# The end of the recurrence turn in another order: mean sums behind the chain, the eight-row state turned in the third tile, the fourth gate by halves

## The chip, the cores and the metric

The kernel runs on one core of a Trainium2 chip. The metric is the device time of one execution in microseconds (us), fp32 data in and out. The times given are medians of a few executions.

## The reference, cut to what matters

The program is one inference step of a hybrid recurrent decoder layer with width 2048. It serves 16 meta tokens with a prompt of 512 tokens, and 8 sample sequences of 4 tokens each: 560 token columns in all. The work that the change touches is the RWKV-7 branch and the gated merge after it:

```python
z = rms_norm(x) @ w_in              # r, k, v, gate za, merge gates ga, gb are column blocks of z
xs = zf + (prev - zf) * mu          # token shift
# per head of 64 channels, per token:
sa = S @ a_t
S = S * w_t + sa * b_t + v_t * k_t  # matrix state
y = S @ r_t
...
mean = mean(y); var = mean((y - mean)**2)          # per head
y = (y - mean) * rsqrt(var + LNX_EPS) * lnx_w + lnx_b
y = (y + bonus) * silu(za)
m = sigmoid(ga) * y + sigmoid(gb) * ob             # ob comes from the GLA branch
x = x + rms_norm(m @ w_out)
```

The final states of the prompt (one) and of the samples (eight) are outputs too.

## The kernel before

All 2048 channels are cut into 16 pairs of heads, 128 channels each. The recurrence stage makes one turn for each pair: `turn_of` is written once for every engine, 15 turns run in a hardware loop (`Fori`) and the last one (`last=True`) stands alone. Every engine works through its own instruction list in order; semaphores (`wait_ge`, `then_inc`) tie the lists together. There is no planner. The order is written by hand.

**The projections are the filling.** Each turn needs six columns tiles of `z`: t = 0 is the key, 1 the receptance r, 2 the value, 3 the gate za, 4 the merge gate ga, 5 the merge gate gb. Tiles 6, 7 and 8 are the key, r and value of the next turn. A tile is a product of 128 weight columns with 560 tokens over 2048 rows, in two token halves of 280. A half has 16 **steps**, and a step (`Projection.steps`, lines 353 to 371) is three matmuls (lines 363, 364, 365), because every fp32 product is split in high and low parts. The parts of the weights are made tile by tile: SyncE loads 1 MB into `raw` in two halves, ScalarE rounds it (`split_hi`, line 341), VectorE subtracts (`split_lo`, line 349). There are two sets of `w_hi` and `w_lo`, used in turn, and one `raw`. Half 0 of a tile always goes to PSUM bank 0 and half 1 to bank 1. Before step 0 of a half, TensorE waits until the half before it in that bank has been read out (`evacuated`), and for the first half also until `split_lo` of the tile is done:

```python
if k == 0:
    pe.wait_ge(self.lo.sem, self.lo.at(i, 2 * t + 2))
    pe.wait_ge(self.evacuated.sem, self.evacuated.at(i, 2 * t - 1 + half))
```

Tiles 0 to 2 and 6 to 8 are read out by ScalarE copies into a shift buffer (`evacuate`, that is `to_shift_buffer`, lines 381, 384, 386); tiles 3 to 5 by ScalarE tanh (`tanh_gate_of`, line 1571) with a VectorE product behind it (lines 1732, 1773, 1810).

**The recurrence stands between the steps.** `run(n)` issues n steps of the filling; between two of them TensorE does a piece of the recurrence whose input the other engines made meanwhile. From the start of tile 4 a turn has 128 steps of filling (tiles 4 to 7); the last turn has 64 (tiles 4 and 5). The order is: the eight sample states (the "eight-row" state) are transposed (line 1903) and copied to `s8` by ScalarE (line 1576); Gram matrices (1923); v transposed (1929); products; a matrix inverse by squarings (1937) with ScalarE copies (1602) and VectorE sums (1766, 1768, 1779, 1782, 1784); the maps (2030, 2040, 2047); the chain over the nine chunks (2071); and the outputs y (2077, 2082).

**The end of the turn**, after y: ScalarE copies y to SBUF (1623, 1625). TensorE forms `s8`'s increment (2089), the sums of y over each head (`head_sums`, 1881, `mean_done`), and the sums of squares (1881 again, `var_done`); VectorE subtracts the mean (1834), ScalarE squares (1631) and takes the root (1646), VectorE divides and merges (1840 to 1850) and GpSimd stores the result. The nine final states are transposed on TensorE (2103), copied by ScalarE (`states_out`, 1639) and stored by GpSimd (1497, 1499). The copies of tiles 6 and 7, the splits of tiles 7 and 8 and the token shift of the next key (`shift_key`, 392 to 400) stand between these.

## Time and profile before

| | before |
|---|---|
| median of 3 runs | 3549.05 us (3548.31 to 3569.71) |
| profiled execution, its own time | 3559.79 us |
| its span, first to last instruction | 3558.3 us |
| TensorE matmul busy | 3279.7 us, 92% |
| VectorE busy | 1721.4 us, 48% |
| ScalarE busy | 1054.2 us, 30% |
| GpSimd busy | 395.8 us, 11% |

A row of the view in order of time gives start, length, engine, line, operation and, in square brackets, how long the engine had been idle and who released it. A row can merge several instructions of one line (x8). The matmul records overlap: one projection matmul is recorded as 0.29 us long and the next starts 0.13 us after it, so that a recorded idle time is shorter than the time lost. Lines that end a wait are those of the instruction that released it. The recurrence stage lies between about 1160 and 3280 us of the span.

### The profile page before, as it was taken

To read this page: it belongs to the slowest core of one execution; us is meant where nothing else is said; L and a number is where in the kernel's file an instruction comes from. 1 tells how busy PE (TensorE), PEld (TensorE's weight loads), DVE (VectorE), ACT (ScalarE), POOL (GpSimd) and SP (SyncE) were. 2 spreads that over 40 slices of the span, in tenths; PEclk is the share of its full clock that TensorE was granted. 3 is DMA by queue.
4 is the path that set the end of the run, shared out by engine and by line. 5 is a ranking of instruction groups with operands and counts; after the bars stand their busy time and mean duration, and the time that the engine had idled before them with its cause. 6 is when DMAs were issued, how large, how long until landed. Compare 5 with 4: busy or idle time off the path is not lost. (4 is left out here: it accounts for less than half of the span.)

```text
span 3558.3 us, 82556 instructions
## 1 busy us (share of the span) xinstructions
PE 3279.7 (92%) x33471; PEld 3028.9 (85%) x33471; DVE 1721.4 (48%) x2447; ACT 1054.2 (30%) x1680; POOL 395.8 (11%) x795
## 2 busy tenths in 40 slices
PE   3899999999997899999999999999999999996796
PEld 3798898898994889988988998998989998895796
DVE  3254454354443445655654654654654654563324
ACT  3232232332320322332332332432332332331222
POOL 2100100100001201110110110110110110111000
PEclk6899898998995999999999999999999999998898
DMA  2222323323313212221221221311221221221422
GB/s 86 71 79 72 125 73 91 119 60 103 106 36 108 71 53 56 74 55 45 75 62 38 74 63 43 80 51 49 75 62 49 64 62 50 61 61 42 150 75 97
DMA packets 368508, 255.10 MB, mean 72 GB/s; under 512 B 19412, under 2 KB 347600, under 8 KB 366288
## 3 DMA queue, kind: packets, MB, share of 16 engines
q1 hardware_dynamic: 342592, 184.18, 18.9%
q0 software_dynamic: 25600, 66.02, 5.8%
q8 instruction: 282, 4.62, 0.5%
q14 instruction: 34, 0.28, 0.0%
HBM read 212.69 MB, written 37.45 MB: 70 GB/s over the span
## 5 line engine op out<-in xcount | busy, mean ns | idle before, releaser
L363 PE MATMUL psum<-act_hi,w_hi 128*128 128x280 f32 (+3 forms) x5216 | 1613.2, 309 | 89.8 <-DVE w_lo L349 38.7
L365 PE MATMUL psum<-act_hi,w_lo 128*128 128x280 f32 (+3 forms) x5216 | 1539.9, 295 | 0.0
L364 PE MATMUL psum<-act_lo,w_hi 128*128 128x280 f32 (+3 forms) x5216 | 1539.1, 295 | 0.0
L363 PEld LDWEIGHTS psum<-act_hi,w_hi 128*128 128x128 f32 (+2 forms) x5216 | 999.6, 192 | 162.7 <-issue 107.0
L364 PEld LDWEIGHTS psum<-act_lo,w_hi 128*128 128x128 f32 (+2 forms) x5216 | 999.0, 192 | 6.0 <-issue 1.0
L365 PEld LDWEIGHTS psum<-act_hi,w_lo 128*128 128x128 f32 (+2 forms) x5216 | 998.3, 191 | 1.1
L349 DVE TENSOR_TENSOR w_lo<-raw,w_hi 128x1024 fp32r<-128x1024 f32 (+1 forms) x326 | 396.6, 1217 | 320.9 <-ACT w_hi L341 306.4
L341 ACT CAST w_hi<-raw 128x1024 fp32r<-128x1024 f32 (+1 forms) x326 | 340.1, 1043 | 87.4 <-DMA raw<-in_w_in_dram 36.5
L1937 PE MATMUL psum<-arena 64*64 64x64 f32 x9216 | 309.4, 219 | 6.6 <-DVE arena L1782 6.5
L1937 PEld LDWEIGHTS psum<-arena 64*64 64x64 f32 x9216 | 286.1, 134 | 32.9 <-issue 32.9
L1497 POOL DMA_DIRECT2D out_s_rwkv_dram<-arena x128 | 78.9, 624 | 1558.5 <-ACT arena L1639 1558.4
L1602 ACT COPY arena<-psum 128x576 f32<-128x576 f32 x80 | 51.4, 643 | 280.6 <-PE psum L1937 280.6
L1571 ACT ACTIVATE arena<-psum 128x280 f32<-128x280 f32 x96 | 39.0, 406 | 307.6 <-PE psum L365 306.6
L677 ACT COPY arena<-psum 128x280 f32<-128x280 f32 x48 | 18.9, 394 | 315.0 <-PE psum L365 314.9
L946 DVE SCALAR_TENSOR_TENSOR arena<-arena,psum 128x512 f32<-128x512 f32 x64 | 47.9, 748 | 101.6 <-PE psum L1214 100.4
L384 ACT COPY arena<-psum 128x248 f32<-128x248 f32 (+1 forms) x50 | 18.4, 367 | 264.7 <-PE psum L365 264.7
L1214 PE MATMUL psum<-arena 48*128 48x512 f32 x128 | 85.2, 798 | 6.5 <-DVE arena L939 6.5
L1815 DVE SCALAR_TENSOR_TENSOR arena<-psum,arena 128x64 f32<-128x64 f32 x128 | 36.3, 284 | 111.2 <-PE psum L2071 111.1
L2254 DVE COPY arena<-psum 128x256 f32 (+1 forms) x32 | 13.6, 425 | 145.7 <-PE psum L2300 145.7
L1203 PEld LDWEIGHTS psum<-arena 128*128 128x128 f32 x512 | 73.5, 227 | 11.8 <-issue 11.8
L635 POOL DMA_DIRECT2D out_s_gla_dram<-arena x32 | 23.0, 718 | 529.8 <-DVE arena L946 529.8
L1463 POOL DMA_DIRECT2D arena<-in_state_rwkv_dram x128 | 75.6, 599 | 47.6 <-issue 43.8
(312 smaller groups left out, 3513.8 us busy)
## 6 DMA issues: line engine op xcount, KB each, us to landing
raw<-in_w_in_dram SPq DMA_DIRECT2D x288, 512.0 KB, 4.6
arena<-in_state_gla_dram POOLq DMA_DIRECT2D x32, 512.0 KB, 5.3
out_s_gla_dram<-arena POOLq DMA_DIRECT2D x32, 512.0 KB, 3.3
raw<-in_w_out_dram SPq DMA_DIRECT2D x32, 512.0 KB, 4.5
ob_dram<-arena POOLq DMA_DIRECT2D x16, 280.0 KB, 3.1
arena<-ob_dram POOLq DMA_DIRECT2D x16, 280.0 KB, 5.8
m_dram<-arena POOLq DMA_DIRECT2D x16, 280.0 KB, 2.4
arena<-m_dram SPq DMA_DIRECT2D x4, 1120.0 KB, 12.2
```

The lines of the kernel that those rows point to most:

```text
L341: nc.scalar.copy(w_hi[t % 2][:, ks, 0:width], raw[half][:, :, 0:width]).then_inc(self.hi.sem, 1)
L349: eng.tensor_tensor(w_lo[t % 2][:, ks, 0:width], raw[half][:, :, 0:width], w_hi[t % 2][:, ks, 0:width].bitcast(F32), SUB).then_inc(self.lo ...
L363: pe.matmul(out, hi, act_hi[:, k, cols], start=(k == 0), stop=False)
L364: pe.matmul(out, hi, act_lo[:, k, cols], start=False, stop=False)
L365: mm = pe.matmul(out, lo, act_hi[:, k, cols], start=False, stop=(k == KT - 1))
L946: stt(out=sstate[s % 3][:, n, :], in0=sstate[s % 3][:, n, :], scalar=ends[:, n, GN + s:GN + s + 1], in1=bank[4 + n], op0=MUL, op1=ADD).the ...
L1203: m = mm(o8[n][:, TAIL + s * TS:TAIL + (s + 1) * TS], sstate[s % 3][:, k, kv(n)], q_8[k][:, s * TS:(s + 1) * TS], start=False, stop=False, ...
L1214: m = mm(bank[4 + n], kd_seq[0:LAST, kv(n)], v_rows[0:LAST, GF, :], start=True, stop=True)
L1463: pool.dma_start(state8_in[0:C, s, :].rearrange("v (h k) -> v h k", h=2), state_rwkv[0, s, ds(2 * i, 2)].rearrange("h v k -> v h k")).then ...
L1497: pool.dma_start(s_rwkv[0, s, ds(2 * i, 2)].rearrange("h v k -> v h k"), state_out[0:C, s, :].rearrange("v (h k) -> v h k", h=2)).then_inc ...
L1602: nc.scalar.copy(out, psum[:, b:b + 2, :].rearrange("p b x -> p (b x)")[:, 0:NC * C].rearrange("p (c t) -> p c t", c=NC)).then_inc(signal. ...
L1937: m = mm(out, left(c)[head[h]], right(c)[head[h]], start=True, stop=True)
```

## The change

It reorders; it adds and removes no arithmetic.

- **Third tile.** On TensorE the eight state transposes move from behind all 32 steps of tile 3 to behind its step 16, that is between its two halves. ScalarE copies them to `s8` between the two tanh of that tile.
- **Fourth gate by halves.** ScalarE takes the tanh of tile 4's half 0 earlier, behind the second of three copies of the inverse, and half 1 at the old place. VectorE does the product of half 0 behind the third sum of the inverse (`gate_second(0)`), and half 1 behind the fourth.
- **End of the turn, TensorE.** Before: 4 steps, s8 product, 10 steps, mean sums, 20 steps, 8 of 9 state transposes, square sums, 6 steps, the last transpose, the other 13 steps. After: 6 steps, mean sums, s8 product, 8 steps, square sums, 14 steps, 8 transposes, 6 steps, the last one, the other 19 steps.
- **End of the turn, ScalarE.** Before: y copies, split 7, read-out of tile 6, square, split 8, states 0 and 1, root, state 2, read-out of tile 7. After: split 7, y copies, square, root, read-out of tile 6, split 8, states 0, 1, 2, read-out of tile 7.
- **End of the turn, VectorE.** Before: s8 sum and scaling, split 7, centring, split 8, key shift, division and merge. After: centring, split 7, s8, division and merge, split 8, key shift.

```diff
--- before.py
+++ after.py
@@ -1565,16 +1565,17 @@
                     act.wait_ge(exps.sem, exps.next(i))
                     pd.split_hi(act, i, mine, 4)
 
-                    def tanh_gate_of(t, out):
-                        for half in range(2):
+                    def tanh_gate_of(t, out, halves=(0, 1)):
+                        for half in halves:
                             act.wait_ge(pd.half.sem, pd.half.at(i, 2 * t + half + 1))
                             nc.scalar.activation(out[:, half * HALF:(half + 1) * HALF], bank[half][:, 0:HALF], ACT.Tanh, scale=0.5).then_inc(tanh_gate.sem, 1)
                             act.wait_ge(tanh_gate.sem, tanh_gate.next(i))
-                    tanh_gate_of(3, tg)
-
+                    tanh_gate_of(3, tg, (0,))
                     act.wait_ge(s8_turned.sem, s8_turned.at(i, 1))
                     nc.scalar.copy(s8, bank[6].rearrange("p (s v) -> p s v", s=NSEQ)).then_inc(s8_ready.sem, 1)
                     act.wait_ge(s8_ready.sem, s8_ready.next(i))
+                    tanh_gate_of(3, tg, (1,))
+
                     for g in range(3):
                         act.wait_ge(v_turned.sem, v_turned.at(i, g + 1))
                         cs, src = (slice(4 * g, 4 * g + 4), bank[4 + g]) if g < 2 else (slice(NF, NC), bank[4][:, 0:P])
@@ -1605,7 +1606,9 @@
                     for n, out in enumerate((x2, n_d, x2)):
                         act.wait_ge(inv_mm.sem, inv_mm.at(i, n + 1))
                         to_sbuf(out, 6, inv_a)
-                    tanh_gate_of(4, tg)
+                        if n == 1:
+                            tanh_gate_of(4, tg, (0,))
+                    tanh_gate_of(4, tg, (1,))
                     if not last:
                         pd.split_hi(act, i, mine, 6)
                     for n in range(2):
@@ -1618,34 +1621,34 @@
                     nc.scalar.copy(uv[0:C, :, 0:C], pq[:, :, C:P]).then_inc(p_ready.sem, 1)
                     act.wait_ge(p_ready.sem, p_ready.next(i))
                     tanh_gate_of(5, tg)
+                    if not last:
+                        pd.split_hi(act, i, mine, 7)
                     act.wait_ge(y_state.sem, y_state.at(i, 1))
                     act.wait_ge(stored.sem, stored.at(i, 0))
                     nc.scalar.copy(y_t[:, 0:NF * C], bank[7]).then_inc(mine.sem, 1)
                     act.wait_ge(mine.sem, mine.next(i))
                     nc.scalar.copy(y_t[:, NF * C:T], bank[6][:, C:C + LAST]).then_inc(y_ready.sem, 1)
                     act.wait_ge(y_ready.sem, y_ready.next(i))
-                    if not last:
-                        pd.split_hi(act, i, mine, 7)
-                        evacuate(act, i, mine, 6)
                     act.wait_ge(centred.sem, centred.at(i, 1))
                     nc.scalar.activation(e_t, y_t, ACT.Square).then_inc(squared.sem, 1)
                     act.wait_ge(squared.sem, squared.next(i))
-                    if not last:
-                        pd.split_hi(act, i, mine, 8)
-
-                    def states_out(n):
-                        act.wait_ge(out_turned.sem, out_turned.at(i, n + 1))
-                        w = 4 if n < 2 else 1
-                        nc.scalar.copy(state_out[0:C, 4 * n:4 * n + w, :], bank[2 + n % 2][0:C, 0:w * P].rearrange("p (s k) -> p s k", s=w)).then_inc(out_read.sem, 1)
-                        act.wait_ge(out_read.sem, out_read.next(i))
-                    states_out(0)
-                    states_out(1)
                     act.wait_ge(var_done.sem, var_done.at(i, 1))
                     for half in range(2):
                         signal = root if half else mine
                         nc.scalar.activation(e_t[:, half * HALF:(half + 1) * HALF], bank[6 + half][:, 0:HALF], ACT.Sqrt,
                                              scale=1.0 / HEAD, bias=tiny[:, 1:2]).then_inc(signal.sem, 1)
                         act.wait_ge(signal.sem, signal.next(i))
+
+                    def states_out(n):
+                        act.wait_ge(out_turned.sem, out_turned.at(i, n + 1))
+                        w = 4 if n < 2 else 1
+                        nc.scalar.copy(state_out[0:C, 4 * n:4 * n + w, :], bank[2 + n % 2][0:C, 0:w * P].rearrange("p (s k) -> p s k", s=w)).then_inc(out_read.sem, 1)
+                        act.wait_ge(out_read.sem, out_read.next(i))
+                    if not last:
+                        evacuate(act, i, mine, 6)
+                        pd.split_hi(act, i, mine, 8)
+                    states_out(0)
+                    states_out(1)
                     states_out(2)
                     if not last:
                         evacuate(act, i, mine, 7)
@@ -1760,18 +1763,21 @@
 
                         op(slice(0, NC), lambda b: psum[:, b:b + 2, :].rearrange("p b x -> p (b x)")[:, 0:NC * C].rearrange("p (c t) -> p c t", c=NC)).then_inc(signal.sem, 1)
                         dve.wait_ge(signal.sem, signal.next(i))
+                    def gate_second(half):
+                        dve.wait_ge(tanh_gate.sem, tanh_gate.at(i, half + 3))
+                        pd.evacuated.count = 8 + half
+                        cols = slice(half * HALF, (half + 1) * HALF)
+                        stt(out=gate[:, cols], in0=tg[:, cols], scalar=1.0, in1=gate[:, cols], op0=ADD, op1=MUL).then_inc(pd.evacuated.sem, 1)
+                        dve.wait_ge(pd.evacuated.sem, pd.evacuated.next(i))
                     for n in range(4):
                         dve.wait_ge(inv_mm.sem, inv_mm.at(i, n + 1))
                         if n < 2:
                             both(lambda c, b: dve.tensor_copy((t2, t_d)[n][:, c, :], b(4)), inv_b)
                         if n > 0:
                             both(lambda c, b: tt(inv[:, c, :], inv[:, c, :], b(2), ADD), inv_b)
-                    for half in range(2):
-                        dve.wait_ge(tanh_gate.sem, tanh_gate.at(i, half + 3))
-                        pd.evacuated.count = 8 + half
-                        cols = slice(half * HALF, (half + 1) * HALF)
-                        stt(out=gate[:, cols], in0=tg[:, cols], scalar=1.0, in1=gate[:, cols], op0=ADD, op1=MUL).then_inc(pd.evacuated.sem, 1)
-                        dve.wait_ge(pd.evacuated.sem, pd.evacuated.next(i))
+                        if n == 2:
+                            gate_second(0)
+                    gate_second(1)
                     if not last:
                         pd.split_lo(dve, i, mine, 6)
                     for n in range(2):
@@ -1819,14 +1825,6 @@
                     for h in range(2):
                         tt(uv8[h], bc(uv[:, NF, 64 * h:64 * h + 64], NSEQ), member[:, 1:].unsqueeze(2).to_broadcast([P, NSEQ, C]), MUL).then_inc(uv8_ready.sem, 1)
                         dve.wait_ge(uv8_ready.sem, uv8_ready.next(i))
-                    dve.wait_ge(s8_done.sem, s8_done.at(i, 1))
-                    tt(s8_new, s8, bank[3].rearrange("p (s v) -> p s v", s=NSEQ), ADD).then_inc(mine.sem, 1)
-                    dve.wait_ge(mine.sem, mine.next(i))
-                    tt(s8_new, s8_new, decays[:, NC:NC + NSEQ].unsqueeze(2).to_broadcast([P, NSEQ, C]), MUL).then_inc(s8_next.sem, 1)
-                    dve.wait_ge(s8_next.sem, s8_next.next(i))
-                    if not last:
-                        pd.split_lo(dve, i, mine, 7)
-
                     dve.wait_ge(mean_done.sem, mean_done.at(i, 1))
                     for half in range(2):
                         cols = slice(half * HALF, (half + 1) * HALF)
@@ -1834,8 +1832,12 @@
                         stt(out=y_t[:, cols], in0=bank[4 + half][:, 0:HALF], scalar=-1.0 / HEAD, in1=y_t[:, cols], op0=MUL, op1=ADD).then_inc(signal.sem, 1)
                         dve.wait_ge(signal.sem, signal.next(i))
                     if not last:
-                        pd.split_lo(dve, i, mine, 8)
-                        shift_key(i, mine, 6)
+                        pd.split_lo(dve, i, mine, 7)
+                    dve.wait_ge(s8_done.sem, s8_done.at(i, 1))
+                    tt(s8_new, s8, bank[3].rearrange("p (s v) -> p s v", s=NSEQ), ADD).then_inc(mine.sem, 1)
+                    dve.wait_ge(mine.sem, mine.next(i))
+                    tt(s8_new, s8_new, decays[:, NC:NC + NSEQ].unsqueeze(2).to_broadcast([P, NSEQ, C]), MUL).then_inc(s8_next.sem, 1)
+                    dve.wait_ge(s8_next.sem, s8_next.next(i))
                     dve.wait_ge(root.sem, root.at(i, 1))
                     dve.reciprocal(e_t, e_t).then_inc(mine.sem, 1)
                     dve.wait_ge(mine.sem, mine.next(i))
@@ -1850,6 +1852,8 @@
                     stt(out=y_t, in0=y_t, scalar=0.25, in1=ob, op0=MUL, op1=ADD).then_inc(merged.sem, 1)
                     dve.wait_ge(merged.sem, merged.next(i))
                     if not last:
+                        pd.split_lo(dve, i, mine, 8)
+                        shift_key(i, mine, 6)
                         mine.close()
                 with dve.Fori(0, LAST_TURN) as i:
                     turn_of(i)
@@ -1894,14 +1898,16 @@
                     pe.wait_ge(rk_ready.sem, rk_ready.at(i, 1))
                     pe.sem_inc(waited.sem, 1)
                     head_sums(sq, 2, rk_sum)
-                    for _ in fill:
-                        pass
-
+                    for _ in range(4):
+                        next(fill)
                     pe.wait_ge(load_s8.sem, load_s8.at(i, 16 * NSEQ))
                     pe.sem_inc(waited.sem, 1)
                     for s in range(NSEQ):
                         m = tr(bank[6][:, s * C:(s + 1) * C], state8_in[0:C, s, :], ident[0:C, 0:C])
                     m.then_inc(s8_turned.sem, 1)
+                    for _ in fill:
+                        pass
+
 
 
                     fill = chain(*(pd.steps(pe, i, t) for t in ((4, 5) if last else (4, 5, 6, 7))))
@@ -2082,17 +2088,20 @@
                             m = mm(bank[6][head[h], C + at:C + at + TS], s8[head[h], s, :], a_r[head[h], NF, C + at:C + at + TS], start=False,
                                    stop=(s == NSEQ - 1), skip_group_check=True)
                     m.then_inc(y_state.sem, 1)
-                    run(4)
+                    run(6)
+                    pe.wait_ge(y_ready.sem, y_ready.at(i, 1))
+                    pe.sem_inc(waited.sem, 1)
+                    head_sums(y_t, 4, mean_done)
                     for h in range(2):
                         pe.wait_ge(uv8_ready.sem, uv8_ready.at(i, h + 1))
                         pe.sem_inc(waited.sem, 1)
                         m = mm(bank[3][head[h], :], gram[:, NF, h, 0:C], uv8[h], start=True, stop=True)
                     m.then_inc(s8_done.sem, 1)
-                    run(10)
-                    pe.wait_ge(y_ready.sem, y_ready.at(i, 1))
-                    pe.sem_inc(waited.sem, 1)
-                    head_sums(y_t, 4, mean_done)
-                    run(20)
+                    run(8)
+                    pe.wait_ge(squared.sem, squared.at(i, 1))
+                    pe.sem_inc(waited.sem, 1)
+                    head_sums(e_t, 6, var_done)
+                    run(14)
                     pe.wait_ge(s8_next.sem, s8_next.at(i, 1))
                     pe.sem_inc(waited.sem, 1)
 
@@ -2104,9 +2113,6 @@
                         m.then_inc(out_turned.sem, 1)
                     turn_states(0)
                     turn_states(1)
-                    pe.wait_ge(squared.sem, squared.at(i, 1))
-                    pe.sem_inc(waited.sem, 1)
-                    head_sums(e_t, 6, var_done)
                     run(6)
                     pe.wait_ge(out_read.sem, out_read.at(i, 1))
                     pe.sem_inc(waited.sem, 1)
```

## Rows read from the trace of the kernel before

**Rows 1.** The page, part 1: busy us, share of the span, instructions.

```profile
PE 3279.7 (92%) x33471; PEld 3028.9 (85%) x33471; DVE 1721.4 (48%) x2447; ACT 1054.2 (30%) x1680; POOL 395.8 (11%) x795
```

**Rows 2.** Waits of TensorE: line <- releaser: us in total, times, longest.

```profile
PE psum L363 <- DVE arena L1773: 13.6, 16, 0.9
PE psum L1923 <- ACT arena L1576: 13.1, 16, 0.8
PE psum L1937 <- DVE arena L1782: 6.5, 15, 0.4
```

**Rows 3.** Order of time, TensorE, end of tile 3 in a turn (start, us).

```profile
2139.86 0.29 PE L365 MATMUL psum<-act_hi,w_lo 128*128 128x280 f32 x1
2140.08 0.71 PE L1903 MATMUL psum<-ident,arena 64*128 64x64 f32 x8
2141.61 0.49 PE L1923 MATMUL psum<-arena 64*128 64x128 f32 x4 [0.82 <-ACT arena L1576]
```

**Rows 4.** GpSimd in order of time, and line 1463 alone: loads of the states.

```profile
2116.25 4.80 POOL L1463 DMA_DIRECT2D arena<-in_state_rwkv_dram  x8 [2.95 <-issue]
...
DMA to landing us min/median/max: 2.0/2.8/6.1
```

**Rows 5.** Order of time, TensorE, where tile 5 starts, a turn earlier.

```profile
2043.82 0.40 PE L363 MATMUL psum<-act_hi,w_hi 128*128 128x280 f32 x1 [0.85 <-DVE arena L1773]
...
2049.28 0.53 PE L1937 MATMUL psum<-arena 64*64 64x64 f32 x11 [0.42 <-DVE arena L1782]
```

**Rows 6.** Order of time, ScalarE and VectorE, the same stretch.

```profile
2043.57 2.13 ACT L341 CAST w_hi<-raw 128x1024 fp32r<-128x1024 f32 x2 [0.16 <-ACT arena L1571]
...
2044.73 2.48 DVE L349 TENSOR_TENSOR w_lo<-raw,w_hi 128x1024 fp32r<-128x1024 f32 x2 [0.39 <-ACT w_hi L341]
...
2048.13 0.75 DVE L1782 TENSOR_TENSOR arena<-arena,psum 128x576 f32<-128x576 f32 x1
```

**Rows 7.** Order of time, TensorE, end of the same turn.

```profile
2083.25 0.40 PE L363 MATMUL psum<-act_hi,w_hi 128*128 128x280 f32 x1
...
2084.99 1.08 PE L2089 MATMUL psum<-arena 128*64 128x512 f32 x4
2086.01 0.40 PE L363 MATMUL psum<-act_hi,w_hi 128*128 128x280 f32 x1
...
2089.98 1.11 PE L1881 MATMUL psum<-arena,head_ones 128*128 128x280 f32 x4
2090.72 0.50 PE L363 MATMUL psum<-act_hi,w_hi 128*128 128x280 f32 x1
2091.06 0.29 PE L364 MATMUL psum<-act_lo,w_hi 128*128 128x280 f32 x1
```

**Rows 8.** Order of time, ScalarE, end of the same turn.

```profile
2100.71 1.28 ACT L1646 ACT_TABLE_LOAD   x1 [0.18 <-PE psum L1881]
2102.01 1.02 ACT L1646 ACTIVATE arena<-psum,tiny 128x280 f32<-128x280 f32 x2
...
2103.57 0.39 ACT L381 COPY arena<-psum 128x280 f32<-128x280 f32 x1 [0.16 <-ACT arena L1639]
...
2109.30 0.76 ACT L1540 ACTIVATE arena<-arena,params 128x560 f32<-128x560 f32 x1 [0.60 <-ACT arena L386]
```

**Rows 9.** Order of time, VectorE, end of the same turn.

```profile
2096.46 2.48 DVE L349 TENSOR_TENSOR w_lo<-raw,w_hi 128x1024 fp32r<-128x1024 f32 x2 [4.32 <-ACT w_hi L341]
...
2100.97 0.26 DVE L400 SCALAR_TENSOR_TENSOR arena<-arena,params 128x32 f32<-128x32 f32 x1
2103.13 3.65 DVE L1840 RECIPROCAL arena<-arena 128x560 f32<-128x560 f32 x1 [1.91 <-ACT arena L1646]
...
2109.94 0.74 DVE L1850 SCALAR_TENSOR_TENSOR arena<-arena 128x560 f32<-128x560 f32 x1
```

**Rows 10.** Order of time, TensorE, end of the last turn.

```profile
3258.52 1.97 PE L2089 MATMUL psum<-arena 128*64 128x512 f32 x4
3260.42 2.00 PE L1881 MATMUL psum<-arena,head_ones 128*128 128x280 f32 x4
```

## The prediction

> **What bounds the kernel.** I read the page's busy shares first: TensorE's matmuls fill 92% of the span and no other engine half of it [rows 1]. So only TensorE's lost time, or a longer path between two of its pieces, can move the result. The table of its waits then names the places in the recurrence turns [rows 2]. Three matter here: the first step of tile 5 waits for the gate product (16 times, 0.85 us each), the first Gram matmul waits for the copy of the eight-row state (16 times, 0.82), and the second product of the inverse waits for a VectorE sum (15 times, 0.43). The change aims at the first two. The end of the turn has no such row: there every wait is covered by steps of the filling. The third view, the engines in order of time over one turn, tells what is queued behind what.
>
> A projection matmul is recorded as 0.29 us and the next starts 0.13 after it. So the time lost at a step is the recorded idle plus 0.16, where the wait is all that stands there.
>
> **Part 1: eight-row state in the third tile.** Before: last matmul of tile 3 at 2139.86, transposes at 2140.08, first Gram matmul at 2141.61 [rows 3]; 1.75 us between filling and Gram matmuls. After: the transposes stand between the halves of tile 3, and 16 steps (48 matmuls of 0.13, 6.2 us) cover ScalarE's copy. They still cost their place. Starting them costs 0.22 instead of 0.13. Eight take 0.71 to the end of the last record of about 0.2, so the next matmul can start after about 0.56. The restart of the filling costs some 0.1 (its first gap is 0.34 instead of 0.13 behind another kind of matmul [rows 7], so between 0 and 0.21). That is 0.09 + 0.56 + 0.1 = 0.75, and then 0.22 to the Gram matmul: 0.97 against 1.75, a gain of 0.78 a turn, **12.5 us** in 16. Bounds: 0.4 (a dearer restart on both sides) and 0.97 (the whole wait, 0.82 + 0.16). The state's loads must land earlier now. GpSimd issues them from 2116.25 to 2121.05 and the slowest landing took 6.1 us [rows 4], so by 2127.2. The transposes move to about 2140.1 − 6.2 = 2133.9. They stay covered by 6.7 us. On ScalarE the copy slides between two tanh; tile 4 needs neither before the Gram matmuls are through.
>
> **Part 2: fourth gate by halves.** The wait at 2043.82 goes: tile 5's step 0 needs only gate half 0, which is now ready well before. Lost there: 0.85 + 0.16 = 1.0 a turn. But what is late next? TensorE runs to the inverse's second product at 2049.28, where it waited 0.42 for line 1782 [rows 5]. That sum stands at 2048.13, behind split 6 on VectorE (2044.73, 2.48 long, itself waiting for ScalarE's split), and ScalarE's split starts at 2043.57 straight behind the tanh of half 1 [rows 6]. That tanh waits for the last step of tile 4's half 1, which lies *before* the wait that goes. So the path (last step of tile 4, tanh of half 1, split on ScalarE, split on VectorE, sum 1782, second product) keeps its length, and TensorE merely arrives 1.0 earlier and waits 1.4 instead of 0.4. I cost this edit at **0** in the 15 turns of the loop. The bound on the other side is 1.0 each. The last turn has no split 6 (the wait for line 1782 is counted 15 times, not 16 [rows 2]); there the gain of **1.0 us** stays.
>
> **Part 3: end of the turn.** TensorE's pieces are the same, with four breaks in the filling before and after. So only new waits count. I count on from the start of the filling behind y, 2083.25, with the pieces' lengths of rows 7. Thirty matmuls take 2089.98 − 2086.01 = 3.97, 0.132 each.
> - run(6): 18 × 0.132 = 2.38, mean sums start 2085.63. The s8 product starts 0.74 later (2090.72 − 2089.98) at 2086.37, the filling 1.02 later (2086.01 − 2084.99) at 2087.39.
> - run(8): 24 × 0.132 = 3.17, square sums start 2090.56. Centring and square, three short operations, have had over 3.8 us from the end of the mean sums (2086.74): no wait. The square sums end 1.11 later, 2091.67; the filling restarts at 2091.30.
> - Now seven steps of run(14), and then **step 0 of tile 7**, which needs tile 6's half 0 read out of bank 0. It is wanted at 2091.30 + 0.34 + 20 × 0.13 = 2094.24.
> - Before, ScalarE read that half out long ahead of the root. Now the read-out stands behind it in ScalarE's queue, so the chain runs: square sums end 2091.67, 0.1 handover (2103.03 to 2103.13 in rows 8 and 9), table load and root 2100.71 to 2103.03 = 2.32, gap 0.16, copy 0.39, handover 0.1 [rows 8]. 2091.67 + 3.07 = 2094.74.
>
> That is a new wait of **0.50 us** a turn, 7.5 us in 15 turns. It shows as about 0.35 of recorded idle before line 363, released by ScalarE line 381. The difference of two near-equal paths is uncertain: from 0 (the read-out just fits) up to twice that, 1.0. ScalarE's queue behind it is only shifted: the read-out of half 1, split 8, the three state copies. Tile 7's half 1 starts 6 us later and has its bank by then.
>
> The row shows the table load at 1.28 and the root starting 0.02 behind it [rows 8]. The Trainium skill (ScalarE: Activation LUTs, What ACT_TABLE_LOAD costs) gives 1.28 for the load too, but adds a drain of about 1.38, 2.66 us for each switch. By that the wait would be 1.88 us and the change a loss; no row of this chain shows such a drain, and the sum goes by the rows.
>
> What else is queued behind the moved work: VectorE now divides before split 8 and the key shift. Root done 2094.1, division and merge 7.55 (2103.13 to 2110.68), split 8 and key shift 4.77 (2096.46 to 2101.23) [rows 9] after it: done by about 2106.7 with gaps. ScalarE wants the key at 2109.30, shifted by the new wait to 2109.8 [rows 8]: 3 us in hand. Split 8 itself is ready by 2104.4, and TensorE needs it only in the next turn. SyncE's load of the next turn's tile 3 waits for split 8 and so is issued some 5.5 us later; issued at about 2103 it is wanted only several ScalarE operations behind the square of 2109.30, so I count it as hidden. On GpSimd the state stores are still issued ahead of the saves and of the merged rows, all a little earlier. Cost of all these: 0; if the cover of the key went, the excess over 3 us would fall on the next turn.
>
> **Last turn.** There is no filling left, so the end is a bare chain. The s8 product (3258.52, on to 3260.42) no longer stands ahead of the mean sums, and the eight transposes no longer ahead of the square sums [rows 10]. At full speed the product is 1.02 [rows 7]; y's copy ends before it does, so about **1.0 us** is gained (0.5 to 1.9).
>
> **Sum.** −12.5 − 1.0 + 7.5 − 1.0 = −7.0 us. On the profiled execution, 3559.8, that is 3552.8. It was 10.7 slower than the median, an offset of the run and not of the turn's waits, so from the median of 3549 I forecast **3542 us**.
>
> **Rivals.**
> - *The halves pay (chance 0.10).* If the path by split 6 has slack that I don't see, the 1.0 of part 2 stays in each loop turn: 15 us more, 3527. For it: the wait at the gate is real and the largest in rows 2. Against it: the 0.42 at line 1782 shows that this path ended last before.
> - *The read-out fits (0.15).* No wait at tile 7: 7.5 more, 3534.5. For it: my two paths are 3 us long and differ by half a microsecond.
> - *The root's chain costs more (0.12), and it is slower than before.* At step 0 of tile 7 the break-even wait is 14.5 / 15 = 0.97 us. If the switch to the root takes one more 1.28 than rows 8 show in the place where nothing covers it, the wait is 1.78 and 26.7 us stand against 14.5 gained: +12, 3561. For it: before, other copies preceded the load. Against it: the load follows the sums at once in rows 8, and the root it. The skill's drain would be this case.
> - *The state's move gains nothing (0.08).* Something right behind it (the tanh of half 1 and its product, now later on VectorE) holds the Gram stage as long: −2.0 + 7.5, 3554.5.
> - *The forecast: 0.55*, on its own 3535 to 3550 by the bounds of the terms.
>
> The range 3527 to 3560 holds all but the third rival and the edges of the others. One per cent, 35.5 us, is about what a measurement of this kernel tells from no change; no case comes near, so within 1% gets 0.92. Faster 0.03 and slower 0.05 are for an error in the reading, a lost cover in each turn of over 2.4 us above all.
>
> **What would show it.** Right: the waits for lines 1576 and 1773 are gone from TensorE's table; the wait for line 1782 is near 1.3 us, 15 times; a new one at line 363 for ScalarE line 381, 0.2 to 0.5 us, 15 times; the turn's period shorter by 0.2 to 0.4 us. Wrong: line 1782 still at 0.43 (then the halves paid), no row for line 381, or TensorE waiting at the start of a turn for the key or at tile 3 for the states' loads.

## The result, and the profile after

The changed kernel takes 3602.3 us (median of 4 runs, 3599.1 to 3609.0). Against runs of the kernel before on the same chip (median 3555.8) the ratio is **1.012**, 95% interval 1.0101 to 1.014: it is slower by about 43 us by the ratio, 46.5 by the medians. I had forecast 3542, range 3527 to 3560, and given "slower by over 1%" a chance of 0.05. The profiled execution has a span of 3607.5 us against 3558.3.

TensorE's waits after, the view of [rows 2] (us in total, times, longest):

```profile
PE psum L1879 <- issue: 47.7, 14, 4.5
...
PE psum L1943 <- DVE arena L1788: 23.1, 15, 1.6
...
PE psum L363 <- ACT arena L381: 4.4, 15, 0.3
```

The kernel before had in that view, of rows not shown yet:

```profile
PE psum L1875 <- issue: 26.0, 14, 2.3
```

Line 1788 after is line 1782 before, and 1879 is 1875, the first product of a turn. The two waits at which the change aimed are gone (no row for the state's copy nor for the gate's product). What I had costed came as costed: the inverse's second product waits 1.54 us instead of 0.43, 15 times, and the new wait for the read-out (line 381) is there 15 times, 0.29 us each. What I had not costed at all is the first row: the idle at the jump from a turn's end back to its start grew from 26.0 to 47.7 us over 14 jumps. "issue" means that no semaphore is what it waits for.

I cut every turn of the two traces at the starts of the same matmuls (medians over the turns in the loop, us; the jump is counted from 0.13 behind the start of the last filling matmul, where the next would start):

| stretch of a turn | before | after |
|---|---|---|
| last filling matmul to first product of the next turn (the jump) | 1.97 | 3.33 |
| first product to the first head sums | 6.57 | 8.21 |
| to the second head sums (r k) | 13.28 | 13.28 |
| to the first Gram matmul | 10.34 | 9.60 |
| to the transposes of b, k | 16.40 | 16.41 |
| to the product behind the inverse | 32.88 | 32.88 |
| to y's products | 20.51 | 20.51 |
| y's products (3.49) and on to the last filling matmul | 28.28 | 28.82 |

Three of my terms can be read off: the state's move gives 0.74 (I said 0.78), the halves give 0.00, the end of the turn costs 0.54 (I said 0.50). The loss is in the first two rows, 3.0 us a turn.

The second row has no new wait in it. In most turns after the change, TensorE runs at its lower level of 1.2 GHz there. Of the ten microseconds behind the jump that is shown further down, 3.4 were at that level (PE, PEld, DVE, ACT and POOL busy, then the mean granted clock, DMA share and GB/s):

```profile
2141.00:2151.00 10.00, 10.00 (x56) 9.14 (x57) 5.61 (x7) 6.08 (x8) 5.27 (x9) 0.83 0.19 58
```

The same matmul of line 1875 has a median of 399 ns before and of 609 ns after:

```profile
L1875 PE MATMUL psum<-lora,arena x128: 397/399/674, 1194.5 to 3157.0; 96*128 96x280 f32 x128
```

```profile
L1879 PE MATMUL psum<-lora,arena x128: 397/609/807, 1195.3 to 3208.6; 96*128 96x280 f32 x128
```

(min, median and max ns.) In the 15 turns of the loop the granted clock stood at the lower level for 17.1 us before and for 85.3 us after; a low stretch began at or right behind 3 of 14 jumps before and behind 12 after. At half the clock the 68 us more cost about half of that, 34 (an estimate). Not all of them are at the jump. All low stretches of the loop stand at one of two places, right behind a jump or right behind y's small products, some 104 us into the turn: 10.2 and 6.8 us before, 51.2 and 34.1 us after.

**Why the jump is longer.** This is the DMA traffic around one jump of each kernel. First before, the two microseconds that end with the last filling matmul (2107.79), and the 2.1 from there to the first product. The line "DMA" is the busy share in tenths in 40 slices; q1 carries the weight loads, q0 the states, q8 the instructions:

```profile
DMA  0096962000000093742900000092903000000091
...
q0 software_dynamic: 100, 0.11, 31.5%
q8 instruction: 1, 0.02, 3.7%
```

```profile
DMA  9230000209893201000000098752000000099620
...
q0 software_dynamic: 117, 0.12, 31.4%
```

After, the two microseconds that end with the last filling matmul (2137.30), and the 3.6 to the first product:

```profile
DMA  9999999999999999899899788788999987889999
...
q1 hardware_dynamic: 1067, 0.54, 98.5%
q0 software_dynamic: 61, 0.06, 8.3%
```

```profile
DMA  9999999793332222232101010000000000000000
...
q1 hardware_dynamic: 391, 0.19, 17.9%
q0 software_dynamic: 148, 0.15, 12.7%
q8 instruction: 1, 0.02, 1.7%
```

The one packet of q8 is 16 KB of code, fetched for the jump: in all 14 jumps of both kernels, and in those of every run below, the first product starts 1.8 to 2.1 us behind the end of that packet (median 1.9), wherever the packet lies. So its end sets the length of the jump. TensorE's sequencer reaches the branch 2.06 us before the last filling matmul starts, in both kernels. Before, the packet starts about 1.0 us ahead of that matmul in 12 jumps of 14 (0.3 in the others); the weight load had ended 4 us ahead of it. After, the packet starts 0.3 to 1.9 us *behind* it, while the weight load's packets run until 1.0 to 1.8 behind. The load is that of the next turn's tile 3. SyncE issues it when VectorE has done split 8, and that I had seen move:

```profile
2130.29 0.74 DVE L1852 SCALAR_TENSOR_TENSOR arena<-arena 128x560 f32<-128x560 f32 x1
2131.07 1.23 DVE L349 TENSOR_TENSOR w_lo<-raw,w_hi 128x1024 fp32r<-128x1024 f32 x1
```

```profile
2132.53 1.63 SPq L332 DMA_DIRECT2D raw<-in_w_in_dram  x2
```

```profile
2137.30 0.29 PE L365 MATMUL psum<-act_hi,w_lo 128*128 128x280 f32 x1
2140.92 0.94 PE L1879 MATMUL psum<-lora,arena 96*128 96x280 f32 x3 [3.33 <-issue]
```

(VectorE, SyncE's queue and TensorE in order of time, one turn.) The halves of split 8 now end 5.0 and 3.7 us ahead of the last filling matmul, and each sends half a megabyte on its way. The load's first packets start 3.7 us ahead of that matmul; before, it was 8.8.

### The profile page after: what moved, and what is told of

Same layout as the page of the kernel before. It is cut to its first block and busy times, and to the rows that moved or that the text cites. A ratio compares the mean times of both kernels' runs of the same rounds, so it can differ in the third digit from the quotient of the medians.

```text
span 3607.5 us, 82556 instructions
## 1 busy us (share of the span) xinstructions
PE 3313.2 (92%) x33471; PEld 3051.3 (85%) x33471; DVE 1721.9 (48%) x2447; ACT 1053.1 (29%) x1680; POOL 385.3 (11%) x795
## 5 line engine op out<-in xcount | busy, mean ns | idle before, releaser
L1943 PE MATMUL psum<-arena 64*64 64x64 f32 x9216 | 309.4, 219 | 23.2 <-DVE arena L1788 23.1
L1879 PE MATMUL psum<-lora,arena 96*128 96x280 f32 x128 | 49.6, 551 | 47.7 <-issue 47.7
L2260 DVE COPY arena<-psum 128x256 f32 (+1 forms) x32 | 13.6, 425 | 148.1 <-PE psum L2306 148.1
L1879 PEld LDWEIGHTS psum<-lora,arena 96*128 96x128 f32 x128 | 30.9, 252 | 58.7 <-issue 50.4
```

The costliest lines, as they stand in the source:

```text
L1879: m = mm(bank[2 + 2 * n + half][:, 0:HALF], lora_w[n][0:LORA, :], lora[n][:, half * HALF:(half + 1) * HALF], start=True, stop=True)
L1943: m = mm(out, left(c)[head[h]], right(c)[head[h]], start=True, stop=True)
```

## The experiments

Ratios are to the kernel before, run on the same chip beside each; intervals are 95%.

**The end's order alone.** The kernel before with the change's edits of the turn's end on all three engines; of TensorE's:

```diff
-                    run(4)
+                    run(6)
+                    pe.wait_ge(y_ready.sem, y_ready.at(i, 1))
+                    pe.sem_inc(waited.sem, 1)
+                    head_sums(y_t, 4, mean_done)
...
-                    run(10)
...
-                    run(20)
+                    run(8)
+                    pe.wait_ge(squared.sem, squared.at(i, 1))
+                    pe.sem_inc(waited.sem, 1)
+                    head_sums(e_t, 6, var_done)
+                    run(14)
```

> The kernel before with the reordered end of the turn alone (state transposes and fourth gate as before). Traffic theory (VectorE's late split 8 lets the 1 MB load of the next turn's tile 3 lie over TensorE's jump back, the jump's code fetch waits for it, and the longer idle drops TensorE to 1.2 GHz): all of the loss and none of the gain of the state's move, so 12 us slower than the changed kernel, ratio to before about 1.016; gap at the jump 3.3 us or more against 1.9, new wait at tile 7 0.5 us. Rival (the loss comes from the state's transposes or the gate halves, or from all three together): ratio near 1.00.

Measured: 1.0127 (1.0089 to 1.0164), median 3608.9 us. The jump's idle is 44.8 us over 14 (against 26.0), the low clock 68 us in the loop, the read-out's wait is there 15 times:

```profile
PE psum L1873 <- issue: 44.8, 14, 4.1
```

The whole loss is in this part. I had expected 1.016. In the two profiles the loop is as long as in the changed kernel (2011.8 us against 2011.7): the state's move is missing, but the low clock is 17 us shorter, behind y's products, and the jumps' idle 3 us.

**The other two parts alone.**

The kernel before with the change's edits of the third tile and of the gate halves:

```diff
-                    tanh_gate_of(3, tg)
-
+                    tanh_gate_of(3, tg, (0,))
...
+                    tanh_gate_of(3, tg, (1,))
...
-                    for _ in fill:
-                        pass
-
+                    for _ in range(4):
+                        next(fill)
```

> The kernel before with the state transposes in the third tile and the fourth gate by halves, the end of the turn as before. By the sum of my prediction: 0.78 us a turn and 1.0 in the last turn, 13 us faster, ratio 0.996; the wait for the gate gone, the wait for line 1782's sum up from 0.43 to 1.4 us; gap at the jump 1.9 as before. Rival (the halves pay): 28 us faster, 0.992. Rival (the loss is here): ratio above 1.00.

Measured: 0.997 (0.9953 to 0.9988).

```profile
PE psum L1881 <- issue: 26.0, 14, 2.2
...
PE psum L1945 <- DVE arena L1788: 23.1, 15, 1.5
```

The jump is as before, the gate's wait has moved whole into the inverse's: 23.1 against 6.5 [rows 2], while the stretch around both is 32.87 us against 32.88. The halves alone gain nothing in a loop turn. The low clock took 30.7 us instead of 17.1, which gave back 7 of the 11 us that the state's move gained in the loop.

**Late split 8 in the kernel before.** Two places on VectorE:

```diff
-                    if not last:
-                        pd.split_lo(dve, i, mine, 8)
-                        shift_key(i, mine, 6)
                     dve.wait_ge(root.sem, root.at(i, 1))
...
                     dve.wait_ge(merged.sem, merged.next(i))
+                    if not last:
+                        pd.split_lo(dve, i, mine, 8)
+                        shift_key(i, mine, 6)
```

> The kernel before with one edit: VectorE does split 8 and the key shift behind the division and the merge. TensorE's and ScalarE's lists are untouched. Traffic theory: the load of the next turn's tile 3 is issued about 12 us later than before (the division starts late here) and lies over the jump or behind it; if over it, the gap grows from 1.9 to 3 us or more and the clock falls at most jumps, 30 to 50 us slower, ratio 1.008 to 1.014. The key may also be late for ScalarE here, up to 5 us a turn on top. Rival (TensorE's own new order or its new wait at tile 7 is what costs): ratio 1.000 and gap 1.9.

Measured: 1.0298 (1.0258 to 1.0337), more than expected and by another way.

```profile
PE psum L363 <- DVE w_lo L349: 58.7, 16, 28.7
PE psum L1880 <- DVE arena L1704: 46.4, 16, 3.7
...
PE psum L1874 <- issue: 25.4, 14, 2.2
```

Here the division starts late, so split 8 comes so late that the load falls wholly *behind* the jump (around the jump that ends at 2147.3 SyncE issues it at 2149.7), and the jump is as short as before (25.4). The lost time is real waits: for a low half of weights (58.7 us, 38.7 in the kernel before) and for the second head sums, since key and weights are late in the next turn. The low clock, 95.6 us in the loop, makes up the rest. So late split 8 does not by itself lengthen the jump; the traffic over the jump must do it.

**Early split 8 in the changed kernel.**

```diff
+                    if not last:
+                        pd.split_lo(dve, i, mine, 8)
+                        shift_key(i, mine, 6)
                     dve.wait_ge(root.sem, root.at(i, 1))
...
-                        pd.split_lo(dve, i, mine, 8)
-                        shift_key(i, mine, 6)
```

> The changed kernel with split 8 and the key shift back ahead of the division on VectorE, nothing else. Traffic theory: the load is issued by 2100 on the clock of the old turn and is done before the jump; gap at the jump back to about 2.0 us, low clock behind the jump in 2 to 4 turns of 15 instead of 14, the state's 12 us gained and the wait at tile 7 (8 us) kept: ratio to before 0.998, about 50 us faster than the changed kernel. Rival (TensorE's order): stays at 1.012.

Measured: 1.001 (0.9992 to 1.0028). The loss is gone with this edit alone.

```profile
PE psum L1880 <- issue: 27.5, 14, 2.3
...
PE psum L363 <- ACT arena L381: 4.4, 15, 0.3
```

The low clock is 41.0 us in the loop, less than 85.3, more than 17.1; by half of the 24 us more, 12, the 15 turns are longer than my sum for this kernel. That, and no new wait, is why the 0.998 was not reached in this profile.

**The load over the jump, and nothing else changed.** This edits SyncE's list alone, in the kernel before:

```diff
                     for t in range(3, 9):
+                        if t == 3:
+                            sp.wait_ge(out_read.sem, out_read.at(i, 0))
                         load(i, t)
```

> The kernel before with one more wait, on SyncE alone: the load of tile 3 of the next turn is held until the ninth state has been copied, some 4 us ahead of TensorE's jump back (before it was issued some 10 us ahead of it). All compute engines keep their lists, and the load still lands long before its split is due. Traffic theory: the 1 MB lies over the jump as in the changed kernel; code fetch begins 0.3 to 2 us after the last filling matmul instead of 1 us before it, gap at the jump from 2.1 to 3.3 us or more, low clock behind most jumps, ratio 1.008 to 1.012. Rival (the order of the compute engines costs): ratio 1.000.

Measured: 1.0149 (1.0128 to 1.0169), median 3609.4 us. The kernel has the compute engines' order of before and the loss of after; it is somewhat more than the 1.008 to 1.012 that I expected. (The edit has the same wait ahead of the last turn's load.)

```profile
PE psum L1879 <- issue: 52.8, 14, 3.9
```

Around one jump, the two microseconds that end with the last filling matmul (2123.34) and the 4.1 behind it:

```profile
q1 hardware_dynamic: 1251, 0.63, 106.2%
q0 software_dynamic: 32, 0.03, 4.7%
```

```profile
q0 software_dynamic: 256, 0.26, 25.8%
q1 hardware_dynamic: 540, 0.27, 24.5%
q8 instruction: 1, 0.02, 1.6%
```

The code packet again comes behind the last matmul, about 1 us after it. The jump's median is 3.93 us, the low clock 68 us in the loop, 54.6 of it behind the jumps, in 14 of 14.

**The load held past the jump in the changed kernel.**

```diff
                     for t in range(3, 9):
+                        if t == 3:
+                            sp.wait_ge(low_done.sem, low_done.at(i, 2))
                         load(i, t)
```

> The changed kernel, orders of all compute engines untouched, SyncE's load of the next turn's tile 3 held until TensorE has done the first products of the new turn. Split 8 stays late, the traffic leaves the jump. Traffic theory: gap back to about 2.1 us, low clock behind the jump rare, ratio to before 1.001 as with the early split 8; unless ScalarE's split of tile 3 now comes late (it is due some 5 us behind the first products, the load takes as long), which would add 0 to 1 us a turn. Rival (late split 8 or the new order of the compute engines hurts in itself): stays at 1.012.

Measured: 1.0057 (1.0035 to 1.0078), some 23 us faster than the changed kernel with split 8 as late as there, but not the 1.001 that I expected.

```profile
PE psum L1883 <- issue: 26.4, 14, 2.2
...
PE psum L1889 <- DVE arena L1711: 7.6, 9, 1.2
```

The jump is short again. The second row is the price that I had allowed for, the late split of tile 3, 0.5 us a turn on average; the low clock of 64.8 us in the loop is the rest, and behind the short jumps it still fell in 7 turns.

**Reading out ahead of the root**, on top of the early split 8 (the last argument is the half):

```diff
+                    if not last:
+                        evacuate(act, i, mine, 6, 0)
                     act.wait_ge(var_done.sem, var_done.at(i, 1))
...
-                        evacuate(act, i, mine, 6)
+                        evacuate(act, i, mine, 6, 1)
```

> The kernel with the early split 8, and ScalarE copies tile 6's half 0 out of its bank ahead of the wait for the square sums instead of behind the root. My reading of the end of the turn: the wait at tile 7's first step (0.54 us a turn) goes, everything else stays, 8 us less than with the early split 8 alone, ratio to before 0.999. Rival (that stall only reappears at another step): no gain.

Measured: 0.9957 (0.9943 to 0.9971), median 3543.2 us. There is no row for line 381 any more; the end of the turn is 24.77 us against 25.33 behind y's products, 0.56 a turn. That is 8 us, as expected. That the ratio is 0.9957 and not 0.999 I had not foreseen: in the profiles the rest is the clock (6.8 us low in the loop instead of 41.0, worth some 17), and nothing in the edit says why.

**Split 6 spread**, on top of that:

```diff
-                    if not last:
-                        pd.split_lo(dve, i, mine, 6)
                     for n in range(2):
...
                         both(lambda c, b: tt(t2[:, c, :], t2[:, c, :], b(6), ADD), inv_b)
+                        if not last:
+                            pd.split_lo(dve, i, mine, 6, halves=(n,))
```

> The kernel of the run before it, and VectorE no longer does split 6 between the gate and the inverse's sums: its two halves stand behind the first and second sum of line 1782. My reading: the wait of 1.5 us for that sum, into which the gate's wait had gone, is worth 1.5 to 1.7 us a turn; 22 us less than without it, ratio to before 0.993. Rival (the path by split 6 is not what holds line 1782's sum, or the split now delays the next sum as much): under 5 us.

Measured: 0.9927 (0.9905 to 0.995), median 3536.1 us. The stretch of the inverse is 31.26 us against 32.88, so 1.62 a turn, 24 us in all: the path that I named in part 2 was the one that held the halves back. But the kernel is only some 7 to 11 us faster than without it, where I had expected 22; that the ratio is the expected one is luck, since the kernel that it builds on was faster than I had thought. The clock took the rest: 64.8 us low in the loop against 6.8, in 12 turns of 15 at the same place, from some 102 us into the turn. In the two profiles it took all of it, 1948.6 us for the loop against 1947.1.

> The kernel with the spread split 6 once more, unchanged, in five rounds beside the next one. Ratio to before 0.993 as measured. In its first profile TensorE fell to the lower clock level some 102 us into the turn in 11 turns of 15, right behind the 32 four-column products of y, which took back 15 to 20 of the 24 us won at line 1782. If that belongs to the kernel it shows again; if it was chance of one execution it is gone and the profiled span is about 20 us shorter.

Measured: **0.9937** (0.9924 to 0.995), median 3537.8 us; the span of this profile is 3525.7. The low stretch is there again, in 11 turns, 41.0 us in the loop. Four microseconds of it, and the six behind (PE, PEld, DVE, ACT and POOL busy, then the granted clock, DMA share and GB/s):

```profile
2065.00:2069.00 4.00, 4.00 (x23) 3.98 (x23) 0.00 (x0) 0.79 (x2) 0.00 (x0) 0.57 0.00 0
2069.00:2075.00 6.00, 6.00 (x39) 4.63 (x38) 4.39 (x6) 1.07 (x2) 0.00 (x0) 1.00 0.14 32
```

TensorE is busy all through. It has no wait before it either; ahead of it lie y's small products (3.5 us).

```diff
                     for h in range(2):
+                        if h:
+                            run(2)
...
-                    run(6)
+                    run(4)
```

> The same, and two of the six steps of filling behind y's products are moved between its two heads' halves, so that the run of small products is never longer than 1.8 us. If TensorE's low clock at that place comes from the long run of small products: windows there rare, up to 20 us less, ratio 0.988. Rival (the drop does not depend on that place, or was chance): as the kernel beside it within 0.2%. The work and the waits are the same in both.

Here `h` is the head whose y products follow. Measured: 0.9984 (0.9968 to 0.9999), median 3557.1 us: 17 to 19 us *slower* than the kernel beside it, which neither of my expectations had. Two steps between the small products do not keep the clock up; the low level takes 88.7 us in the loop, and again begins behind y's products in 12 turns. My idea that the length of the unbroken run of small products sets the clock falls. What makes the clock fall there in one turn and not in the next stays open.

The low stretches of all profiles, one execution each, counted by the place where they begin:

| kernel | idle at 14 jumps, us | behind a jump: times, us | behind y's products: times, us |
|---|---|---|---|
| before | 26.0 | 3, 10.2 | 2, 6.8 |
| after | 47.7 | 12, 51.2 | 6, 34.1 |
| the end's order alone | 44.8 | 13, 51.2 | 5, 17.1 |
| load over the jump | 52.8 | 14, 54.6 | 4, 13.7 |
| the other two parts alone | 26.0 | 3, 10.2 | 4, 20.5 |
| late split 8 | 25.4 | 4, 20.5 | 11, 41.0 |
| early split 8 | 27.5 | 4, 13.7 | 5, 27.3 |
| load held past the jump | 26.4 | 7, 23.9 | 9, 41.0 |
| reading out ahead of the root | 27.1 | 0 | 2, 6.8 |
| split 6 spread | 26.2 | 4, 17.1 | 12, 47.8 |
| split 6 spread, again | 24.1 | 1, 3.4 | 11, 37.5 |
| steps between y's halves | 24.8 | 6, 23.9 | 12, 64.9 |

(Late split 8 has 34.1 us more at a third place, behind its late head sums, 24 to 26 us into the turn.) The times behind a jump go with its idle time: 12 to 14 where the jump is long, 0 to 7 where it is short. Those behind y's products do not.

The best version of all is the one with the spread split 6: 0.9937 of the kernel before.

## Why the prediction was wrong

**Part 1, the state in the third tile: right.** 0.74 us a turn against 0.78. No new wait took its place; the rival with chance 0.08 did not come.

**Part 2, the halves: right.** Cost 0 in the loop. The wait moved by the path that I named, and the run with split 6 spread shows that it was this path, since 1.62 us came free with it.

**Part 3, the new wait at tile 7: right**, 0.54 a turn against 0.50, and 0.56 when it was taken out by itself. The rival of a dearer root (0.12) did not come: the load still takes 1.28 and the root starts 0.01 behind it (line 1638, at 2121.07 and 2122.36), as in [rows 8]. By the figure of the Trainium skill (ScalarE: Activation LUTs, What ACT_TABLE_LOAD costs), which adds a drain, I had estimated a wait of 1.88. The trace shows no such drain, here as before.

**Last turn: right in size.** From its start to the end of the program 400.5 us against 402.9, 2.4 less; my terms for it (0.78, 1.0 and 1.0) give 2.8.

**The step that failed** is in "what else is queued behind the moved work". I followed the moved split 8 to SyncE, computed that the load of tile 3 is "issued some 5.5 us later" (it was 5.1), and counted it at 0 because its *split* is wanted late. I priced a transfer only by who waits for its data. I did not ask what else used the DMA engines at its new time, although the jump lies right there and its own row (line 1875, "issue", 26.0 us over 14 jumps) stood in the table that I had read. What "issue" hid here, the fetch of the turn's first code, goes over the DMA engines too. And no term of my sum had TensorE's clock in it.

What it cost, in the profiled executions, over the 15 turns of the loop (1960.9 us before, 2011.7 after, +50.8):

| term | us |
|---|---|
| idle at 14 jumps, 47.7 − 26.0 | +21.7 |
| lower clock behind the jumps, (51.2 − 10.2) / 2 | +20.5 |
| lower clock behind y's products, (34.1 − 6.8) / 2 | +13.6 |
| wait at tile 7, 15 × 0.54 | +8.1 |
| state's move, 15 × 0.72 (means) | −10.8 |
| sum | +53.1 |

The second term follows from the first: where SyncE alone made the jump long the clock fell behind all 14 jumps instead of 3, and where the jump was short again it fell behind 0 to 7. Together the two are 42 of the 51 us. The third term is not shown to follow from the jump: in the other kernels it goes up and down without it. That the fetch comes late *because* of the load is shown from both sides: one wait on SyncE brings it into the old kernel (1.0149), another takes it out of the new one (1.0057). How the load holds the code packet back was not tried. Its own record is 0.9 to 1.6 us long at the jumps of all kernels, so it starts late and does not run long.

My chances were wrong in another way as well. I wrote that slower by over 1% would need "a lost cover in each turn of over 2.4 us" and gave it 0.05. (With the 7 us that I forecast as gained it is 2.8.) The jump and the clock behind it came to 2.8 a turn, half of it a second effect of a first that I had priced at nothing; the clock behind y's products added 0.9.

## What to carry to other kernels

When a step is moved and a transfer moves with it, look at what lies at its *new* time on the same DMA engines, not only at when its data is wanted; a hardware loop's jump back is such a place, since its code comes by DMA. Keep large loads some microseconds away from it (at the short jumps here they had ended some 4 us ahead of the last filling matmul), or start them behind it. And cost a TensorE gap twice if it is likely to be followed by a stretch at 1.2 GHz: in these runs the clock behind the longer jumps cost about as much as the longer gaps themselves (20.5 us against 21.7).

## What the hardware showed that I had not expected

- A jump back of the loop costs TensorE about 2 us even undisturbed, and 3.2 to 4.8 us with a 1 MB load over it. The 16 KB code packet starts 0.3 to 1.1 us ahead of the last filling matmul when no weight load is in flight, and 0.2 to 1.9 us behind it when one is. The first product follows the packet's end by 1.9 us in both cases.
- TensorE's clock can undo an improvement that is real in the stretch where it was made. The inverse became 24 us shorter over the turns and the kernel about 7 to 11; the low level had come up near the end of the turn, behind y's small products, with TensorE busy and no wait near it. Two profiles of that one kernel had it for 64.8 and 41.0 us in the loop, and spans of 3540.6 and 3525.7.
- A wait that is filled from both sides is worth only what the later path leaves: 1.0 us removed at the gate returned as 1.1 us at the inverse, to 0.01 us in the stretch around both.
